# The end of the gated mixers: where the merged columns are transposed, and the output projection's first tiles

## The chip, the cores and the metric

The kernel runs on one core of a Trainium2 chip, in one launch. The core has TensorE (matmuls and transposes, PE in the profile), VectorE (DVE), ScalarE (ACT), GpSimd (POOL) and SyncE (SP), which here only issues DMAs. Each engine takes its instructions in the order in which they were written, and semaphores order them between engines. The metric is the device time of one execution in microseconds (us).

## The reference

Two residual networks follow each other on 256 tokens of 1,024 features in float32: first two layers with attention or retention between feed-forward blocks, then two layers of a gated mixer and an MLP. Cut to what the change touches, a layer of the second network is:

```
h = rmsnorm(x, g_mix[l])
dq, dk, dv, c_q, c_kv_kr, xq, gate_logits = split(h @ w_in[l])
y_diff = diff_attention(...) @ w_diff_o[l]
y_mla  = latent_attention(...) @ w_mla_o[l]
y_mem  = memory_cross_attention(...) @ w_cross_o[l]
gates = sigmoid(gate_logits + b_gate[l])
merged = gates[:, :, 0] * y_diff + gates[:, :, 1] * y_mla + gates[:, :, 2] * y_mem
x = x + merged @ w_out[l]
u = rmsnorm(x, g_mlp[l]) @ w_mlp1[l]
x = x + square(relu(u)) @ w_mlp2[l]
```

The change concerns `merged @ w_out[l]`, once in each of the two layers.

## The kernel before

**Tiles.** The 256 tokens stand in two halves of 128 rows. A weight matrix is streamed in tiles of 128 x 1,024 numbers. SyncE loads a tile into one of four buffers `w_raw`. ScalarE rounds it to `w_hi` (L1884), and VectorE or GpSimd makes `w_lo` = raw - hi (L2186 on VectorE, L2892 on GpSimd). There are four buffers of each, so a `w_hi` may be written when the tile four places back has been used. That pair of operations is the step `split`. While attention outputs are made and until the stage ends, every even tile's `w_lo` is GpSimd's.

**Blocks.** `block` computes 512 output columns (c is 0 or 1) for both halves, in PSUM banks. Each 128 x 128 piece costs three matmuls (L1605, L1606, L1607): input hi by weight hi, input hi by weight lo, input lo by weight hi. A tile holds two chunks of 128 input features, so it is 2 chunks x 2 halves x 3 = 12 matmuls of 512 columns. `w_mla_o` has 512 rows, so a block of it is two tiles; `w_out` has 1,024, so a block is four.

**Transposed inputs.** The left operand is kept transposed. A `turn` is four transposes on TensorE (L1694) of four chunks of one half, then `xt_hi` on ScalarE (L1914) and `xt_lo` on VectorE (L2214). A matmul waits for `xt_lo` of its chunk and half.

**Merging.** `merge` is called for the three branches in turn, n = 0, 1, 2; the last is `w_mla_o`. For each block and half VectorE multiplies the bank by the gate (L2850, or L2856 into a buffer `tmp`) and, for n = 1 and 2, adds it to `mx_merged` (L2861). The add for n = 2 completes `merged(half, c)`, of which there are four.

**The order.** One list of steps, the plan, is written by generators, and every engine's program goes through it in that order and picks what is its own. `tile` writes the matmuls of a tile, and `tile_used` behind it writes the `split` of the tile four places on. `second_part` is a hook: a pair of a tile count and a function. When the number of tiles reaches that count, `tile` writes the matmuls, then the tile's `split`, and then calls the function. Before, only `feed` uses it, which makes the normed and transposed input of a stage. `last_plain` is the output projection: a block for c = 0 and one for c = 1, and in the next stage the result is added to `x`. After `drive(projections(), ...)` the function `mix` writes the four turns of `mx_merged` and then the projection.

Of the kernel before, what the change touches and what calls it, by code (L numbers as in the profile page):

```python
# [16 lines left out]
P = 128  # L17
SEQ = 256
HALVES = SEQ // P
# [95 lines left out]
def column_blocks(n, start=0):  # L115
    return [(start + c, min(BLOCK, n - c)) for c in range(0, n, BLOCK)]
# [263 lines left out]
def drive(main, side=None, every=1, finish=True, steps=1):  # L380
    n = 0
    while True:
        try:
            next(main)
        except StopIteration as stop:
            result = stop.value
            break
        n += 1
        if side is not None and n % every == 0:
            for _ in range(steps):  # L390
                next(side, None)
    if side is not None and finish:
        for _ in side:
            pass
    return result


class Kernel:
# [869 lines left out]
    def mix(self, layer, _):  # L1268
        a, L, small = self.a, f"{layer}", self.small_of
# [39 lines left out]
        def projections():  # L1309
            part = lambda name, dst, after=(): self.project(self.xt, w_in, D, IN_SIZES[name], dst, IN_AT[name], after)  # L1310
            got["cq"] = yield from part("cq", low[:, :, 0:MLA_QL], self.tok_after[0])
            got["ckv"] = yield from part("ckv", low[:, :, CKV_AT:D], self.tok_after[0])
            got["q"] = yield from part("dq", q)
            for c0, m in column_blocks(D):
                got["k", c0] = yield from self.block(self.xt, w_in, D, IN_AT["dk"] + c0, m)
            got["v"] = yield from part("dv", v)
            yield from need("low_t", "ckt")
            got["mq"] = yield from self.project(low_t, a["w_mla_qb_2"][layer], MLA_QL, MLA_H * MLA_QK, mq)
            got["kv"] = yield from self.project(low_t, a["w_mla_kvb_2"][layer], MLA_KVL, MLA_H * PER_KV, kv, first=MLA_QL // P)
            got["low", "over"] = self.last_tile()  # L1320
            got["xq"] = yield from part("xq", xq, [got["low", "over"]])
            yield from need("qt")
            yield from gate(0)
            yield from need("kt")
            yield from gate(1)
            yield from need("cqt", "mkt")
            yield from gate(2)
            self.xt_after = [self.last_tile()]
            yield from merge(0, 0, diff_t, "w_diff_o_2", D, 0)
            yield from merge(1, 2, mc_t, "w_cross_o_2", CROSS_H * CROSS_D, 4)  # L1330
            yield from merge(2, 1, mc_t, "w_mla_o_2", MLA_H * MLA_V, 0)
# [7 lines left out]
            self.step("next_gain", gi + 2, [("gate_bias", layer, g, HALVES - 1, D - BLOCK)])  # L1339

        merged = self.put("mx_merged" + L, 24, [P, HALVES, D])

        def merge(n, g, xt, name, rows, first):
            while any((int(xt is mc_t), first + i) not in turned_out for i in range(rows // P)):
                yield IDLE
            for half in range(HALVES):
                self.step("sigmoid", layer, g, half, gates[g][:, half, :])
            for c, (c0, m) in enumerate(column_blocks(D)):
                b = yield from self.block(xt, a[name][layer], rows, c0, m, first)
                for half in range(HALVES):  # L1350
                    self.step("merge", layer, n, half, c, b, merged[:, half, c0:c0 + m], gates[g][:, half, c0:c0 + m], g)
# [164 lines left out]
        prepared = together(memory_keys(), diff_keys(), diff_queries(), latent(), latent_keys(), cross_queries(), diff_outputs())  # L1516
        side = self.in_step(prepared, outputs())
        drive(projections(), side, finish=False)
        merged_t = Transposed("merged" + L, *self.xt_parts)

        for c in range(2):
            for half in range(HALVES):
                self.turn(lambda h, s: merged[:, h, s * P:(s + 1) * P], merged_t, half, [(4 * c + j, 4 * c + j) for j in range(4)],
                          [("merged", layer, half, c)], self.xt_after)
        self.tok_after = [[("turned", self.uid)]] * HALVES
        drive(self.last_plain(merged_t, a["w_out_2"][layer], D))


# [1519 lines left out]
```

## Time and profile before

| | us |
|---|---|
| median of 3 runs | 2480.88 |
| lowest and highest | 2477.91 and 2481.13 |
| the profiled execution | 2485.56 |
| its span in the trace | 2484.2 |
| TensorE busy in it | 2396.5 |
| VectorE busy | 1521.6 |
| ScalarE busy | 1187.6 |
| GpSimd busy | 283.8 |

The trace is of the one profiled execution, and its span leaves out 1.4 us around it. Times in it count from the span's start. Matmuls are pipelined, so one is listed as longer than the distance to the next, and a wait is what is left between a modelled end and the next start. The granted clock is 1.00 where TensorE has its full 2.4 GHz and 0.50 at 1.2 GHz. A line such as "[0.99 <-DVE mx_merged L2861]" says that the engine stood idle for 0.99 us until VectorE's write of `mx_merged`. The code's end of mixer 0 lies at 1715 to 1740 us of the span and that of mixer 1 at 2257 to 2282 us.

### The profile page before, as it was taken

The page shows a single profiled execution, that of the slowest core. Times are in us where ns is not written, and L with a number is a line of the kernel's source. Part 1 is how long each engine was busy: PE and PEld are TensorE (multiplying, and loading weights), DVE is VectorE, ACT ScalarE, POOL GpSimd, SP SyncE. Part 2 cuts the span into 40 slices and gives each one's busy share as a digit, 9 for nine tenths or more (in the row PEclk, how much of TensorE's full clock was granted, in tenths as well). Part 3 has the DMA queues.
Part 4 walks back from the last instruction along what each step waited for, and adds up shares of the span by engine and source line. Part 5 has one row for each costly group of instructions (what it writes and reads, how often), then busy time and mean ns, then how long its engine had stood idle before and what let it go on. Part 6 is the DMA issues. An engine that isn't in the chain of part 4 may idle for free.

```text
span 2484.2 us, 34969 instructions
## 1 busy us (share of the span) xinstructions
PE 2396.5 (96%) x14214; PEld 2060.9 (83%) x14214; DVE 1521.6 (61%) x2325; ACT 1187.6 (48%) x1782; POOL 283.8 (11%) x247
## 2 busy tenths in 40 slices
PE   8998999889999999999999998999999998999999
PEld 8986787779979977777898786787998876887997
DVE  6555556776556657666655677655665686656654
ACT  4443454344444445444444455554554555554543
POOL 1100010000000000000000121333100122333000
PEclk9999999999999999999999999999999999999999
DMA  7754544446656555544566554445566553445564
GB/s 225 198 200 152 165 127 139 126 146 193 187 171 186 181 192 177 170 137 152 166 183 212 180 170 129 119 126 166 175 196 203 181 156 117 119 144 161 168 187 146
DMA packets 269424, 411.69 MB, mean 166 GB/s; under 512 B 13770, under 2 KB 141658, under 8 KB 269264
## 3 DMA queue, kind: packets, MB, share of 16 engines
q1 hardware_dynamic: 262400, 389.59, 51.5%
q0 software_dynamic: 6432, 19.28, 2.9%
q8 instruction: 112, 1.84, 0.3%
q10 hardware_dynamic: 432, 0.59, 0.1%
q14 instruction: 48, 0.39, 0.0%
HBM read 408.31 MB, written 1.10 MB: 165 GB/s over the span
## 4 chain that ended last, share of the span: by engine, by line
PE 76%; DVE 14%; ACT 6%; issue 2%; POOL 1%; DMA 0%; SPq 0%; ACTq 0%; DVEq 0%
PE banks L1605 14%; PE banks L1607 14%; PE banks L1606 13%; PE banks L1631 10%; PE banks L1640 9%; PE banks L1632 9%; DVE w_lo L2186 3%; ACT w_hi L1884 3%; PE banks L1754 1%; DVE probs L2373 1%; ACT probs L1992 1%; PE banks L1694 1%; PE banks L1707 1%; POOL stat L2873 1%; DVE mx_merged L2861 1%
## 5 line engine op out<-in xcount | busy, mean ns | idle before, releaser
L2186 DVE TENSOR_TENSOR w_lo<-w_raw,w_hi 128x1024 fp32r<-128x1024 f32 x688 | 837.7, 1224 | 706.2 <-ACT w_hi L1884 703.8
L1884 ACT ACTIVATE w_hi<-w_raw 128x1024 fp32r<-128x1024 f32 (+2 forms) x744 | 776.2, 1049 | 569.1 <-PE banks L1607 420.5
L1631 PE MATMUL banks<-xt_hi,w_hi 128*128 128x256 f32 x1920 | 477.9, 287 | 12.2 <-ACT xt_hi L1914 8.9
L1632 PE MATMUL banks<-xt_hi,w_lo 128*128 128x256 f32 x1920 | 475.4, 282 | 0.0
L1605 PE MATMUL banks<-w_hi,xt_hi 128*128 128x512 f32 (+2 forms) x1088 | 450.7, 414 | 12.1 <-DVE xt_lo L2214 4.4
L1607 PE MATMUL banks<-w_hi,xt_lo 128*128 128x512 f32 (+2 forms) x1088 | 430.2, 395 | 0.0
L1606 PE MATMUL banks<-w_lo,xt_hi 128*128 128x512 f32 (+2 forms) x1088 | 429.9, 395 | 0.0
L1631 PEld LDWEIGHTS banks<-xt_hi,w_hi 128*128 128x128 f32 x1920 | 364.2, 190 | 16.2 <-issue 12.6
L1632 PEld LDWEIGHTS banks<-xt_hi,w_lo 128*128 128x128 f32 x1920 | 367.3, 191 | 0.0
L1640 PE MATMUL banks<-xt_lo,w_hi 128*128 128x256 f32 x1920 | 270.3, 283 | 0.0
L1605 PEld LDWEIGHTS banks<-w_hi,xt_hi 128*128 128x128 f32 x1088 | 208.6, 192 | 60.2 <-issue 8.3
L1607 PEld LDWEIGHTS banks<-w_hi,xt_lo 128*128 128x128 f32 x1088 | 207.9, 191 | 47.9
L1640 PEld LDWEIGHTS banks<-xt_lo,w_hi 128*128 128x128 f32 x1920 | 247.5, 189 | 0.0
L1606 PEld LDWEIGHTS banks<-w_lo,xt_hi 128*128 128x128 f32 x1088 | 209.0, 192 | 44.1 <-issue 3.1
L2873 POOL TENSOR_TENSOR stat<-stat,minus_half 128x1 f32<-128x1 f32 (+2 forms) x60 | 53.4, 896 | 1055.2 <-DVE stat L2273 712.1
L2892 POOL TENSOR_TENSOR w_lo<-w_raw,w_hi 128x1024 fp32r<-128x1024 f32 x56 | 134.1, 2394 | 299.2 <-ACT w_hi L1884 299.2
L1605 PE MATMUL banks<-w_hi,ffn_ht_hi 128*128 128x512 f32 x352 | 140.7, 400 | 0.0
L1607 PE MATMUL banks<-w_hi,ffn_ht_lo 128*128 128x512 f32 x352 | 138.7, 394 | 0.0
L1606 PE MATMUL banks<-w_lo,ffn_ht_hi 128*128 128x512 f32 x352 | 138.1, 392 | 0.0
L1605 PE MATMUL banks<-w_hi,mlp_ht_hi 128*128 128x512 f32 x256 | 102.4, 400 | 0.0
L1607 PE MATMUL banks<-w_hi,mlp_ht_lo 128*128 128x512 f32 x256 | 100.8, 394 | 0.0
L1606 PE MATMUL banks<-w_lo,mlp_ht_hi 128*128 128x512 f32 x256 | 100.4, 392 | 0.0
(399 smaller groups left out, 2825.7 us busy)
## 6 DMA issues: line engine op xcount, KB each, us to landing
w_raw<-in_w_mlp SPq DMA_DIRECT2D x128, 512.0 KB, 3.7
w_raw<-in_w_in SPq DMA_DIRECT2D x104, 512.0 KB, 3.7
w_raw<-in_ffn_w_gate SPq DMA_DIRECT2D x88, 512.0 KB, 4.0
w_raw<-in_ffn_w_up SPq DMA_DIRECT2D x88, 512.0 KB, 4.1
w_raw<-in_ffn_w_down SPq DMA_DIRECT2D x88, 512.0 KB, 3.6
w_raw<-in_attn_w_in SPq DMA_DIRECT2D x72, 512.0 KB, 3.8
w_raw<-in_ret_w_in SPq DMA_DIRECT2D x64, 512.0 KB, 3.8
w_raw<-in_ret_w_out SPq DMA_DIRECT2D x16, 512.0 KB, 3.7
```

Source lines behind the costliest of these rows:

```text
L1605: pe.matmul(bank, xh, wh, start=(c == 0), stop=False)
L1606: pe.matmul(bank, xh, wl, start=False, stop=False)
L1607: mm = pe.matmul(bank, xl, wh, start=False, stop=(c == b.chunks - 1))
L1631: pe.matmul(out[f], hi[:, cols], xh, start=(c == 0), stop=False)
L1632: pe.matmul(out[f], lo[:, cols], xh, start=False, stop=False)
L1640: mm = pe.matmul(out[f], hi[:, cols], xl, start=False, stop=(c == DC - 1))
L1694: mm = pe.transpose(bank[:, j * P:(j + 1) * P], t.src(t.half, s), order)
L1707: mm = pe.transpose(bank[0:z.shape[-1], at:at + P], z, order)
L1884: act.activation(k.w_hi[i % SPLIT][:, 0:m], k.raw[i % RAW][:, 0:m], ACT.Copy).then_inc(*ev.mark(k.w_hi_made, ("w_hi", i)))
L2186: dve.tensor_tensor(lo, raw, hi.bitcast(F32), ALU.subtract).then_inc(*ev.mark(k.w_lo_made, ("w_lo", i)))
L2873: pool.tensor_tensor(out, mean, k.minus_half[:, 0:n], ALU.pow).then_inc(*ev.mark(k.pool_done, name))
L2892: pool.tensor_tensor(lo, raw, hi.bitcast(F32), ALU.subtract).then_inc(*ev.mark(k.w_lo_pool, ("w_lo", i)))
```

## The change

The four turns of `mx_merged` are the same instructions as before, in two pairs at other places. The pair for c = 0 is hooked to the first tile of the last merging block (n = 2, c = 1), so it stands between that block's two tiles. The pair for c = 1 is hooked to the second tile of the output projection. The object `merged_t` and the function that writes a pair move ahead of `merge`. `tok_after`, which says from when `tok` may be written again, is set with each pair, so the last one holds, as before.

```
--- before.py
+++ after.py
@@ -1339,6 +1339,13 @@
             self.step("next_gain", gi + 2, [("gate_bias", layer, g, HALVES - 1, D - BLOCK)])
 
         merged = self.put("mx_merged" + L, 24, [P, HALVES, D])
+        merged_t = Transposed("merged" + L, *self.xt_parts)
+
+        def merged_turned(c):
+            for half in range(HALVES):
+                self.turn(lambda h, s: merged[:, h, s * P:(s + 1) * P], merged_t, half, [(4 * c + j, 4 * c + j) for j in range(4)],
+                          [("merged", layer, half, c)], self.xt_after)
+            self.tok_after = [[("turned", self.uid)]] * HALVES
 
         def merge(n, g, xt, name, rows, first):
             while any((int(xt is mc_t), first + i) not in turned_out for i in range(rows // P)):
@@ -1346,6 +1353,8 @@
             for half in range(HALVES):
                 self.step("sigmoid", layer, g, half, gates[g][:, half, :])
             for c, (c0, m) in enumerate(column_blocks(D)):
+                if n == 2 and c == 1:
+                    self.second_part = len(self.tiles) + 1, lambda: merged_turned(0)
                 b = yield from self.block(xt, a[name][layer], rows, c0, m, first)
                 for half in range(HALVES):
                     self.step("merge", layer, n, half, c, b, merged[:, half, c0:c0 + m], gates[g][:, half, c0:c0 + m], g)
@@ -1516,13 +1525,7 @@
         prepared = together(memory_keys(), diff_keys(), diff_queries(), latent(), latent_keys(), cross_queries(), diff_outputs())
         side = self.in_step(prepared, outputs())
         drive(projections(), side, finish=False)
-        merged_t = Transposed("merged" + L, *self.xt_parts)
-
-        for c in range(2):
-            for half in range(HALVES):
-                self.turn(lambda h, s: merged[:, h, s * P:(s + 1) * P], merged_t, half, [(4 * c + j, 4 * c + j) for j in range(4)],
-                          [("merged", layer, half, c)], self.xt_after)
-        self.tok_after = [[("turned", self.uid)]] * HALVES
+        self.second_part = len(self.tiles) + 2, lambda: merged_turned(1)
         drive(self.last_plain(merged_t, a["w_out_2"][layer], D))
```

In the lists below, names end in the buffer's number: `w_hi_53` to `w_hi_56` with `w_lo_57` to `w_lo_60` are the four weight buffers, `mx_merged_228` is layer 0's merged tensor, `mx_mc_t` is the transposed input of the last merging blocks and `xt` the transposed `mx_merged`. The lines of the changed kernel are three higher, since its code is longer.

TensorE before, from the last matmuls of the merging block's last tile to the projection's first tile:

```order
L1605 MATMUL banks<-w_hi_56,mx_mc_t_hi 128x512
L1606 MATMUL banks<-w_lo_60,mx_mc_t_hi 128x512
L1607 MATMUL banks<-w_hi_56,mx_mc_t_lo 128x512
L1694 MATMUL banks<-ident,mx_merged_228 128x128 x16
L1605 MATMUL banks<-w_hi_53,xt_hi 128x512
L1606 MATMUL banks<-w_lo_57,xt_hi 128x512
L1607 MATMUL banks<-w_hi_53,xt_lo 128x512
```

TensorE now, at the first pair of turns, between the two tiles of the last merging block:

```order
L1608 MATMUL banks<-w_hi_55,mx_mc_t_hi 128x512
L1609 MATMUL banks<-w_lo_59,mx_mc_t_hi 128x512
L1610 MATMUL banks<-w_hi_55,mx_mc_t_lo 128x512
L1697 MATMUL banks<-ident,mx_merged_228 128x128 x8
L1608 MATMUL banks<-w_hi_56,mx_mc_t_hi 128x512
L1609 MATMUL banks<-w_lo_60,mx_mc_t_hi 128x512
L1610 MATMUL banks<-w_hi_56,mx_mc_t_lo 128x512
```

and at the second pair, between the second and the third tile of the projection:

```order
L1608 MATMUL banks<-w_hi_54,xt_hi 128x512
L1609 MATMUL banks<-w_lo_58,xt_hi 128x512
L1610 MATMUL banks<-w_hi_54,xt_lo 128x512
L1697 MATMUL banks<-ident,mx_merged_228 128x128 x8
L1608 MATMUL banks<-w_hi_55,xt_hi 128x512
L1609 MATMUL banks<-w_lo_59,xt_hi 128x512
L1610 MATMUL banks<-w_hi_55,xt_lo 128x512
```

Eight of the sixteen transposes have moved ahead of a tile of twelve matmuls, and the other eight behind two tiles of the projection.

VectorE before, from the last adds for c = 0 (the third row completes half 1) to the next layer of splits:

```order
L2861 TENSOR_TENSOR mx_merged_228<-mx_merged_228,tmp_72 128x512
L2856 TENSOR_TENSOR tmp_73<-banks,mx_gate_210 128x512
L2861 TENSOR_TENSOR mx_merged_228<-mx_merged_228,tmp_73 128x512
L2186 TENSOR_TENSOR w_lo_60<-w_raw_52,w_hi_56 128x1024
L2856 TENSOR_TENSOR tmp_70<-banks,mx_gate_210 128x512
L2861 TENSOR_TENSOR mx_merged_228<-mx_merged_228,tmp_70 128x512
L2856 TENSOR_TENSOR tmp_71<-banks,mx_gate_210 128x512
L2861 TENSOR_TENSOR mx_merged_228<-mx_merged_228,tmp_71 128x512
L2214 TENSOR_TENSOR xt_lo<-banks,xt_hi 128x4x128 x4
L2186 TENSOR_TENSOR w_lo_58<-w_raw_50,w_hi_54 128x1024
L2186 TENSOR_TENSOR w_lo_60<-w_raw_52,w_hi_56 128x1024
```

VectorE now, over the same work:

```order
L2864 TENSOR_TENSOR mx_merged_228<-mx_merged_228,tmp_72 128x512
L2859 TENSOR_TENSOR tmp_73<-banks,mx_gate_210 128x512
L2864 TENSOR_TENSOR mx_merged_228<-mx_merged_228,tmp_73 128x512
L2217 TENSOR_TENSOR xt_lo<-banks,xt_hi 128x4x128 x2
L2189 TENSOR_TENSOR w_lo_60<-w_raw_52,w_hi_56 128x1024
L2859 TENSOR_TENSOR tmp_70<-banks,mx_gate_210 128x512
L2864 TENSOR_TENSOR mx_merged_228<-mx_merged_228,tmp_70 128x512
L2859 TENSOR_TENSOR tmp_71<-banks,mx_gate_210 128x512
L2864 TENSOR_TENSOR mx_merged_228<-mx_merged_228,tmp_71 128x512
L2189 TENSOR_TENSOR w_lo_58<-w_raw_50,w_hi_54 128x1024
L2217 TENSOR_TENSOR xt_lo<-banks,xt_hi 128x4x128 x2
L2189 TENSOR_TENSOR w_lo_60<-w_raw_52,w_hi_56 128x1024
```

Two `xt_lo` now stand ahead of `w_lo_60` (the split of the projection's fourth tile), and the other two stand behind `w_lo_58`, a split that the second tile's use releases.

On ScalarE, in the same way, two `xt_hi` have moved ahead of the split `w_hi_56` (the projection's fourth tile), and the other two stand behind `w_hi_54` of the projection's sixth tile. GpSimd's and SyncE's lists are unchanged.

## Rows read from the trace of the kernel before

**Rows 1.** the page's part 1, TensorE's busy time, share of the span, count
```profile
PE 2396.5 (96%) x14214; PEld 2060.9 (83%) x14214; DVE 1521.6 (61%) x2325; ACT 1187.6 (48%) x1782; POOL 283.8 (11%) x247
```

**Rows 2.** TensorE's waits: us in total, times, longest
```profile
PE banks L1694 <- DVE mx_merged L2861: 6.5, 6, 1.8
```

**Rows 3.** timeline of TensorE, layer 0: start, us busy, what, [idle before]
```profile
1717.95 0.39 PE L1605 MATMUL banks<-w_hi,mx_mc_t_hi 128*128 128x512 f32 x1
...
1720.75 0.60 PE L1694 MATMUL banks<-ident,mx_merged 128*128 128x128 f32 x4
1722.34 0.66 PE L1694 MATMUL banks<-ident,mx_merged 128*128 128x128 f32 x4 [0.99 <-DVE mx_merged L2861]
...
1726.12 0.73 PE L1694 MATMUL banks<-ident,mx_merged 128*128 128x128 f32 x4 [0.67 <-DVE mx_merged L2861]
1726.82 0.77 PE L1605 MATMUL banks<-w_hi,xt_hi 128*128 128x512 f32 x1
```

**Rows 4.** timeline of VectorE, layer 0
```profile
1718.75 0.69 DVE L2861 TENSOR_TENSOR mx_merged<-mx_merged,tmp 128x512 f32<-128x512 f32 x1
...
1720.08 2.20 DVE L2861 TENSOR_TENSOR mx_merged<-mx_merged,tmp 128x512 f32<-128x512 f32 x1
1722.21 1.21 DVE L2186 TENSOR_TENSOR w_lo<-w_raw,w_hi 128x1024 fp32r<-128x1024 f32 x1
...
1725.38 0.69 DVE L2861 TENSOR_TENSOR mx_merged<-mx_merged,tmp 128x512 f32<-128x512 f32 x1
1725.99 2.48 DVE L2214 TENSOR_TENSOR xt_lo<-banks,xt_hi 128x512 fp32r<-128x512 f32 x4
1735.30 1.23 DVE L2186 TENSOR_TENSOR w_lo<-w_raw,w_hi 128x1024 fp32r<-128x1024 f32 x1 [6.84 <-ACT w_hi L1884]
```

**Rows 5.** timeline of GpSimd, layer 0
```profile
1719.36 2.38 POOL L2892 TENSOR_TENSOR w_lo<-w_raw,w_hi 128x1024 fp32r<-128x1024 f32 x1 [2.92 <-ACT w_hi L1884]
```

**Rows 6.** timeline of ScalarE, layer 0
```profile
1718.21 1.07 ACT L1884 ACTIVATE w_hi<-w_raw 128x1024 fp32r<-128x1024 f32 x1 [1.74 <-PE banks L1607]
1721.01 1.06 ACT L1884 ACTIVATE w_hi<-w_raw 128x1024 fp32r<-128x1024 f32 x1 [1.73 <-PE banks L1607]
...
1723.03 0.60 ACT L1914 ACTIVATE xt_hi<-banks 128x512 fp32r<-128x512 f32 x1 [0.48 <-PE banks L1694]
...
1734.21 1.06 ACT L1884 ACTIVATE w_hi<-w_raw 128x1024 fp32r<-128x1024 f32 x1 [1.75 <-PE banks L1607]
```

**Rows 7.** timeline of VectorE, layer 1
```profile
2261.43 2.42 DVE L2861 TENSOR_TENSOR mx_merged<-mx_merged,tmp 128x512 f32<-128x512 f32 x1
```

**Rows 8.** windows: length, busy PE PEld DVE ACT POOL, clock, DMA, GB/s
```profile
1720.75:1726.82 6.07, 2.60 (x18) 1.65 (x16) 6.00 (x8) 2.73 (x4) 0.98 (x1) 0.98 0.72 212
1726.82:1739.57 12.75, 12.75 (x49) 10.20 (x49) 2.87 (x4) 3.78 (x4) 3.81 (x2) 0.88 0.28 85
...
2262.31:2268.46 6.15, 3.14 (x18) 2.26 (x16) 6.08 (x8) 2.74 (x4) 0.99 (x1) 0.79 0.68 218
2268.46:2281.70 13.24, 13.24 (x50) 10.60 (x49) 2.89 (x4) 3.78 (x4) 3.82 (x2) 0.84 0.24 74
```

**Rows 9.** windows over seven hand-overs of stages and the matmuls behind
```profile
211.10:218.53 7.43, 4.71 (x16) 3.59 (x17) 6.64 (x12) 2.26 (x5) 0.21 (x1) 0.73 0.22 72
530.65:538.11 7.46, 4.71 (x36) 4.27 (x37) 6.62 (x11) 2.14 (x3) 0.74 (x2) 1.00 0.21 70
728.86:735.74 6.88, 4.71 (x36) 4.26 (x37) 6.08 (x10) 2.14 (x3) 0.14 (x1) 1.00 0.21 80
926.49:932.72 6.23, 4.71 (x23) 3.63 (x24) 5.43 (x9) 2.14 (x3) 1.74 (x4) 1.00 0.43 158
1196.78:1204.23 7.45, 4.68 (x25) 4.27 (x25) 6.62 (x11) 2.14 (x3) 0.70 (x2) 0.78 0.23 72
1750.98:1757.23 6.25, 4.49 (x24) 4.05 (x23) 5.40 (x8) 2.14 (x3) 0.81 (x1) 0.73 0.34 108
2293.11:2299.35 6.24, 4.49 (x27) 4.05 (x25) 5.39 (x8) 2.14 (x3) 0.80 (x1) 0.78 0.32 102
```

## The prediction

> **What bounds the kernel now.** I read the page first: TensorE is busy 96% of the span [rows 1], so time is won or lost where TensorE waits. The list of its waits puts 6.5 us, in six waits, on the adds that finish `mx_merged` [rows 2]. There are two mixers, so this is one place that occurs twice. I then read TensorE's timeline there, in layer 0 [rows 3]. The last tile of the last block starts at 1717.95 and the next thing TensorE can do stands at 1720.75, so one tile is 2.80 us. Then come four turns of four transposes, the first two at 1720.75 and 1722.34, the last at 1726.12, each but the first behind an add. The output projection begins at 1726.82, 6.07 us after the tile's end.
>
> VectorE says why [rows 4]. It is behind by more than a tile. The adds of the first column block, `merged(0,0)` and `merged(1,0)`, start at 1718.75 and 1720.08, although that block's matmuls ended a tile before 1717.95, at 1715.15. The second of them takes 2.20 us in place of 0.69. GpSimd's low part `w_lo` runs from 1719.36 to 1721.74 [rows 5], and the add ends 0.54 us behind it, at 1722.28. In layer 1 the same add starts at 2261.43 and takes 2.42 us [rows 7], so this repeats. Behind it in VectorE's queue stand a `w_lo`, the merges of the second column block (done at 1726.07) and the four `xt_lo`.
>
> The rest of the cost is TensorE's clock. The windows [rows 8] show the stretch between last tile and projection (6.07 and 6.15 us) and the projection's four tiles behind it, 12.75 us at a mean clock of 0.88 and 13.24 us at 0.84. Four tiles at full clock are 4 x 2.80 = 11.2 us, so the low level of 1.2 GHz cost 1.55 and 2.04 us. From the last tile's end to the end of the four tiles it takes 6.07 + 12.75 = 18.82 us in layer 0 and 6.15 + 13.24 = 19.39 us in layer 1, together 38.21 us. The change is weighed against this.
>
> **The first pair of turns, now ahead of the last tile.** TensorE takes work in program order, so the last tile waits for both turns, and the second turn for `merged(1,0)`. Up to here nothing is changed: GpSimd's `w_lo` depends on the `w_hi` that ScalarE starts at 1718.21, when the tile ahead is used [rows 6], which stays. So I take 1722.28 as it is. The second turn starts at 1722.34, as it does now [rows 3], its four transposes take about 0.5 us (0.60 to 0.73 busy, overlapped by what follows), and the last tile starts at 1722.8 in place of 1717.95: **+4.85 us**. Layer 1 shows the same add ending at 2263.85 and gives 4.83. Before, these 2.80 us of matmuls covered most of the late adds; the change takes that cover away.
>
> In exchange the projection starts right behind the last tile. Its first two tiles need only the first four chunks. `xt_hi` of half 1 takes 0.60 us from 1723.03 [rows 6] and `xt_lo` by another 0.7, near 1724.4, ahead of the last tile's end at 1725.6. So the 6.07 us vanish, and nothing is late there.
>
> **The second pair of turns, behind two tiles of the projection.** Call the last tile's new end 0. `w_lo` of the projection's fourth tile stands ahead of the second merges on VectorE and needs ScalarE's `w_hi`, which starts 0.26 after the tile (1721.01 less 1720.75, [rows 3, 6]) and lets VectorE start 1.09 later (1735.30 less 1734.21, [rows 4, 6]). The merges then take some 2.7 us and the last add would start at 4.4. GpSimd's next `w_lo` would start at 0.26 + 2.80 + 1.15 = 4.2 [rows 5, 6], so this add is held as now: it ends at 4.2 + 2.38 + 0.54 = 7.1. The turns can start at 5.6, when the two tiles end, and the second one at 7.2. That is not what ends last. The tile's own `w_hi` and `w_lo` were put ahead of `xt_hi` and `xt_lo` in both queues: `w_hi` starts 0.26 after the second tile and frees VectorE's `w_lo` at 1.35, which takes 1.21 [rows 4]; `xt_lo` takes 0.62 (2.48 for four, [rows 4]), and TensorE follows 0.06 later. That is 3.24 us, and up to 0.1 more since the held add ends just behind its `w_hi`: **3.3 us** (3.2 to 3.4) in which TensorE does eight transposes. The third tile's `w_hi` and `w_lo` are long made.
>
> From the old end of the last tile to the end of the four tiles it is now 4.85 + 11.2 + 3.3 = 19.35 us a layer at full clock, 38.7 us for both, **+0.5 us**. The two waits that replace the one are together about as long.
>
> **The clock.** What was one stretch of 6 us a layer with little but transposes is two, of 4.85 and 3.3 us. The nearest rows are seven places where a stage hands over to the next, with eight transposes and no other matmul of weights in them [rows 9]. Each row takes in 3.4 us of matmuls behind the hand-over, so the hand-overs are 2.8 to 4.1 us long. Behind four of them the clock falls (means of 0.73, 0.78, 0.73, 0.78), behind three, one of them 4.06 us long (7.46 less 3.40), it doesn't. 7.43 x 0.27, 7.45 x 0.22, 6.25 x 0.27 and 6.24 x 0.22 are 2.0, 1.6, 1.7 and 1.4 us; with the 1.55 and 2.04 above I take 1.65 us for each fall. Both 6 us stretches at this place have a fall in or behind them, so I give the new 4.85 us stretch 0.85 and the 3.3 us stretch 0.57 (4 of 7): 2 x 0.85 + 2 x 0.57 = 2.8 falls. With three it is 38.7 + 3 x 1.65 = 43.65 us against 38.21: **+5.4 us**.
>
> The Trainium skill has a rule that is harder on this change: TensorE: Matmul & The Clock Gate, Part 4: PE-mode transpose, says that transposes don't count as activity for the clock as matmuls do. By it every one of the four stretches is as good as idle and the clock would fall behind all: +7.1 us. The trace agrees only in part, since three of seven such stretches in rows 9 kept 1.00.
>
> **The rivals.**
> - All four stretches cost a fall: 38.7 + 6.6 - 38.21, +7.1 us. For it: rows 9 with 2.85 us already had one. Against it: three stretches without.
> - Only the first stretch of each layer does: 38.7 + 3.3 - 38.21, +3.8 us, within the bound below.
> - Not slower: the clock stays high at three or all of the four places. That is +0.5 to +2.1 us. It decides at how the transposes split the wait: by the times above the longest unbroken wait in any of them is 2.2 us, from the first turn's end near 1720.1 to 1722.34. The same page of the Trainium skill, Why this matters for your kernels, only warns of long unbroken idle gaps, and by it the clock would stay high here. Against it: the two waits of 1.80 us at most [rows 2] that ended in a fall in both layers.
> - The add is not held by GpSimd in its new surroundings. It would end at 1720.08 + 0.69 = 1720.77, and the last tile start 1.5 us earlier, 3.0 us for both: +2.4 us. Everything ahead of the add is unchanged, so I hardly believe it.
> - The change does what its form suggests: the merged columns are ready within the last block. All waits and falls would go, 38.21 less 2 x (11.2 + 2.0 for sixteen transposes) or 12 us at most. For that `merged(1,0)` would have to end by 1717.95, and it ends 4.3 us later.
>
> **How the numbers follow.** The profiled execution is 2485.56 us with a span of 2484.2; its ends are untouched, so differences carry over to the median of 2480.88 us, 4.7 lower. Three falls (forecast): 0.32, 2486.3 us, and its own range is 2484.5 to 2488. All four: 0.25, 2488.0. Two: 0.25, 2484.7. None or one: 0.07, 2481.4 to 2483.0. Add not held: 0.04, 2483.3. Ready in time: 0.07, down to 2469. The measurement tells about 0.2%, 5.0 us, from no change. Slower by more: three quarters of 0.32 (5.4 is just over the bound), nearly all of 0.25 and a sixth of the next, 0.51. Faster by more: 0.07. The rest, 0.42, is within. The range 2481.6 to 2489.3 leaves out the last case and the tails.
>
> **What would show it.** TensorE should show a wait of some 1.4 us and then one of some 2.2 us, both on an add of `mx_merged`, ahead of the last tile of the block; no wait at the projection's first tile; and at its third tile a wait on `xt_lo` of some 1.3 us behind the last turn. VectorE should show `w_lo` ahead of that `xt_lo`. The add of 2.20 us should still be long and end 0.5 us behind GpSimd. The count of stretches at half clock between the last block and the projection's end should be three of four. I am wrong if the adds come earlier than they do now, if the first wait is shorter than 4 us in all, or if the number of falls is another.

## The result and the profile after

| | median us | lowest to highest | executions |
|---|---|---|---|
| before | 2480.51 | 2476.8 to 2485.7 | 6 |
| the change | 2489.72 | 2488.7 to 2490.46 | 6 |

The ratio is 1.0037 with an interval of 1.0024 to 1.0050: the change is slower, by about 9 us. A repeated comparison, with 11 executions of the change against 29 of before (x9 below), gave 1.0019 (1.0011 to 1.0028), 4.7 us. The sign holds in both; the size lies between 3 and 12 us, and both intervals contain 1.0024 to 1.0028, some 6 to 7 us. The prediction said 2486.3 us, within 2481.6 to 2489.3, so the first median is 0.4 us above its range.

The profiled execution of the change took 2490.44 us with a span of 2489.1, 4.9 above the span of before. Its busy times, for [rows 1]:

```profile
PE 2397.9 (96%) x14214; PEld 2062.4 (83%) x14214; DVE 1526.3 (61%) x2325; ACT 1188.4 (48%) x1782; POOL 284.1 (11%) x247
```

The work is the same in number. The waits of TensorE on the adds of `mx_merged`, for [rows 2], have grown from 6.5 to 9.1 us (total, times, longest):

```profile
PE banks L1697 <- DVE mx_merged L2864: 9.1, 6, 2.3
```

TensorE's timeline at the end of mixer 0, for [rows 3] (start, us busy, what, [idle before]):

```profile
1719.17 0.40 PE L1610 MATMUL banks<-w_hi,mx_mc_t_lo 128*128 128x512 f32 x1
1721.06 0.63 PE L1697 MATMUL banks<-ident,mx_merged 128*128 128x128 f32 x4 [1.49 <-DVE mx_merged L2864]
...
1723.75 0.66 PE L1697 MATMUL banks<-ident,mx_merged 128*128 128x128 f32 x4 [2.07 <-DVE mx_merged L2864]
1724.17 0.48 PE L1608 MATMUL banks<-w_hi,mx_mc_t_hi 128*128 128x512 f32 x1
...
1727.05 0.40 PE L1608 MATMUL banks<-w_hi,xt_hi 128*128 128x512 f32 x1
...
1734.26 0.66 PE L1697 MATMUL banks<-ident,mx_merged 128*128 128x128 f32 x4 [1.00 <-DVE mx_merged L2864]
...
1736.09 0.47 PE L1608 MATMUL banks<-w_hi,xt_hi 128*128 128x512 f32 x1 [1.17 <-DVE xt_lo L2217]
```

Two waits, 1.49 and 2.07, stand ahead of the last tile of the block (1724.17). The projection starts at 1727.05 without a wait. Its third tile waits 1.17 for `xt_lo`, behind a turn that has itself waited 1.00. That is the shape that the prediction drew. VectorE shows the reason of each, for [rows 4]:

```profile
1721.55 2.15 DVE L2864 TENSOR_TENSOR mx_merged<-mx_merged,tmp 128x512 f32<-128x512 f32 x1
...
1731.59 2.62 DVE L2864 TENSOR_TENSOR mx_merged<-mx_merged,tmp 128x512 f32<-128x512 f32 x1
1734.13 1.21 DVE L2189 TENSOR_TENSOR w_lo<-w_raw,w_hi 128x1024 fp32r<-128x1024 f32 x1
1735.27 1.27 DVE L2217 TENSOR_TENSOR xt_lo<-banks,xt_hi 128x512 fp32r<-128x512 f32 x2
```

and GpSimd, for [rows 5]:

```profile
1720.80 2.35 POOL L2895 TENSOR_TENSOR w_lo<-w_raw,w_hi 128x1024 fp32r<-128x1024 f32 x1 [2.90 <-ACT w_hi L1887]
...
1731.26 2.39 POOL L2895 TENSOR_TENSOR w_lo<-w_raw,w_hi 128x1024 fp32r<-128x1024 f32 x1 [8.11 <-ACT w_hi L1887]
```

Both long adds end behind GpSimd: at 1723.70, 0.55 after 1723.15, and at 1734.21, 0.56 after 1733.65. `w_lo` at 1734.13 stands ahead of `xt_lo` at 1735.27.

ScalarE's `w_hi` mark the tiles' ends (0.26 us before them, as in [rows 6]):

```profile
1719.67 1.06 ACT L1887 ACTIVATE w_hi<-w_raw 128x1024 fp32r<-128x1024 f32 x1 [1.74 <-PE banks L1610]
1727.31 1.06 ACT L1887 ACTIVATE w_hi<-w_raw 128x1024 fp32r<-128x1024 f32 x1 [2.26 <-PE banks L1610]
1732.93 1.06 ACT L1887 ACTIVATE w_hi<-w_raw 128x1024 fp32r<-128x1024 f32 x1 [1.74 <-PE banks L1610]
```

The first two are 7.64 apart, of which a tile is 2.80, so the first wait costs 4.84. The second tile of the projection ends at 1732.93 - 0.26 = 1732.67 and the third starts at 1736.09: 3.42 us.

The windows that answer to [rows 8] run from the last tile's old end, 2.80 behind the first `w_hi` less 0.26, to the end of the projection's four tiles, in layer 0 and in layer 1 (length, busy PE PEld DVE ACT POOL, clock, DMA share, GB/s):

```profile
1722.21:1741.79 19.58, 15.87 (x73) 12.65 (x74) 10.86 (x11) 6.04 (x8) 4.75 (x3) 1.00 0.40 126
2264.57:2288.09 23.52, 19.83 (x72) 15.70 (x73) 10.84 (x11) 5.92 (x7) 4.74 (x3) 0.78 0.34 104
```

Layer 0 never left the full clock and took 19.58 us, against 18.82 before with its fall in it. Layer 1 took 23.52 against 19.39. The waits there are alike (1.25, 2.30, 0.98 and 1.17), so nearly all of the 3.94 us between the layers is the low level of the clock. It stood there in two stretches, the first and the third of these rows:

```profile
2264.20:2271.80 7.60, 5.69 (x16) 4.67 (x17) 3.15 (x3) 0.84 (x2) 1.31 (x1) 0.55 0.40 126
2271.80:2281.80 10.00, 7.85 (x37) 6.09 (x36) 8.06 (x8) 4.26 (x5) 2.39 (x1) 0.99 0.36 108
2281.80:2285.00 3.20, 3.20 (x8) 2.44 (x8) 0.00 (x0) 0.00 (x0) 0.00 (x0) 0.50 0.50 158
```

**One measure for all kernels.** For the experiments I take the whole place, in each layer: from the first matmul on `mx_mc_t`, where the second of the three branches begins to be merged, to the first matmul of the next stage. Before, the change, and each of them a second time (x10, x9); the rows stand in the order before, x10, change, x9, two layers each:

```profile
1698.35:1753.83 55.48, 50.26 (x218) 39.62 (x216) 34.19 (x36) 24.27 (x27) 20.18 (x9) 0.97 0.52 160
2239.92:2295.95 56.03, 51.28 (x217) 40.63 (x216) 34.27 (x36) 24.16 (x27) 20.19 (x9) 0.94 0.52 159
```

```profile
1698.83:1754.41 55.58, 50.31 (x217) 39.66 (x216) 34.20 (x36) 24.27 (x27) 20.19 (x9) 0.97 0.51 160
2240.57:2296.71 56.14, 51.36 (x218) 40.66 (x216) 34.30 (x36) 24.16 (x27) 20.19 (x9) 0.94 0.52 158
```

```profile
1699.81:1756.04 56.23, 48.75 (x217) 38.45 (x216) 36.17 (x36) 24.27 (x27) 20.12 (x9) 1.00 0.51 158
2242.17:2302.35 60.18, 52.72 (x218) 41.50 (x216) 36.16 (x36) 24.15 (x27) 20.15 (x9) 0.91 0.48 148
```

```profile
1697.96:1757.07 59.11, 51.65 (x217) 40.72 (x216) 36.16 (x36) 24.26 (x27) 20.13 (x9) 0.94 0.49 151
2241.70:2302.00 60.30, 52.86 (x217) 41.60 (x216) 36.15 (x36) 24.15 (x27) 20.14 (x9) 0.92 0.50 147
```

Both layers together are 111.5 and 111.7 us before, 116.4 and 119.4 with the change. The first difference, 4.9, is also the difference of the two spans, so the rest of the program took the same time in sum; not in each part, since the stretch ahead of the place is 1.46 us longer with the change (1699.81 against 1698.35) and the one behind it 1.50 shorter (186.75 against 188.25). The spans of the second pair differ by 5.3 (2490.3 and 2485.0), so there the rest took 2.4 us less. The second difference, 7.7, has the same waits (1.48, 2.08, 0.98, 1.17 in layer 0) and differs from the first by what the clock did in layer 0, 1.00 there and 0.94 here. x9 has four low stretches, behind or in each pair's wait in both layers, where the first trace has two, both in layer 1:

```profile
1721.90:1725.40 3.50, 3.50 (x11) 2.97 (x12) 1.24 (x2) 0.60 (x1) 0.00 (x0) 0.53 0.51 150
1734.90:1738.90 4.00, 3.18 (x8) 2.54 (x9) 1.27 (x3) 0.28 (x1) 0.00 (x0) 0.57 0.75 243
2264.00:2271.60 7.60, 5.96 (x17) 4.85 (x18) 2.88 (x3) 0.60 (x1) 1.03 (x1) 0.55 0.36 116
2281.40:2284.80 3.40, 3.40 (x10) 2.71 (x9) 0.00 (x0) 0.00 (x0) 0.00 (x0) 0.52 0.54 153
```

### The profile page after: what moved, and what is told of

The parts are those of the page before. It is cut to its first block, busy times and chain, and to the rows that moved or that the text cites. A ratio compares the mean times of both kernels' runs of the same rounds, so it can differ in the third digit from the quotient of the medians.

```text
span 2489.1 us, 34969 instructions
## 1 busy us (share of the span) xinstructions
PE 2397.9 (96%) x14214; PEld 2062.4 (83%) x14214; DVE 1526.3 (61%) x2325; ACT 1188.4 (48%) x1782; POOL 284.1 (11%) x247
## 4 chain that ended last, share of the span: by engine, by line
PE 76%; DVE 14%; ACT 6%; issue 2%; POOL 1%; DMA 0%; SPq 0%; ACTq 0%; DVEq 0%
PE banks L1608 14%; PE banks L1610 13%; PE banks L1609 13%; PE banks L1635 9%; PE banks L1634 9%; PE banks L1643 9%; DVE w_lo L2189 3%; ACT w_hi L1887 3%; PE banks L1757 1%; DVE probs L2376 1%; ACT probs L1995 1%; PE banks L1697 1%; PE banks L1710 1%; DVE mx_merged L2864 1%; POOL stat L2876 1%
```

## The experiments

The medians are compared with executions of the kernel before on the same chip in the same session: 25 in the first (median 2487.46), 35 in the second (2484.71), 29 in the third (2483.56). x1 to x4 are of the first, x5 to x8 of the second, x9 to x12 of the third, and the three sessions ran on three chips. A difference in us is the ratio less one, times 2483. "Place" is the sum of the measure above over both layers, against 111.5 to 111.7 before.

**x1, only the first pair moved.** The second pair stands ahead of the whole projection:

```
-        self.second_part = len(self.tiles) + 2, lambda: merged_turned(1)
+        merged_turned(1)
         drive(self.last_plain(merged_t, a["w_out_2"][layer], D))
```

> The first pair of turns stands in the last merging block, as in the change; the second pair stays ahead of the whole projection, as before. Theory of the queues: the last tile starts 4.85 us later, as in the change, and the projection's first tile then waits for the last add (0.26 + 1.09 for w_hi, then w_lo and the four merging operations, 5.1 us) and its turn, 5.65 us. From the old end of the last tile to the end of four tiles that is 4.85 + 5.65 + 11.2 = 21.7 us a layer at full clock against 17.3 before, +8.9 us for both layers, and with two falls of the clock more than before +12 us; in any case slower than the change by 4 to 5 us. Rival, that the clock's falls are the whole loss and each pair brings its own: half of the change's loss, +4.6 us.

2500.87 us, ratio 1.0054 (1.0037 to 1.0070), +13.4; place 125.2, at clocks 0.92 and 0.89. The first wait of the change is there, and so is the old one, now of 3.79 us and at the low level of the clock (four transposes took 1.11 us in place of 0.66):

```profile
1734.70 1.11 PE L1697 MATMUL banks<-ident,mx_merged 128*128 128x128 f32 x4 [3.79 <-DVE mx_merged L2864]
```

As expected. The first pair pays for itself only if the projection can then start at once.

**x2, only the second pair moved.**

```
-                if n == 2 and c == 1:
-                    self.second_part = len(self.tiles) + 1, lambda: merged_turned(0)
...
+        merged_turned(0)
         self.second_part = len(self.tiles) + 2, lambda: merged_turned(1)
```

> The first pair stays behind the last merging block and its merges, as before; the second pair stands behind two tiles of the projection, as in the change. Theory of the queues: the first tile of the projection still waits 6.0 us, since its xt_lo stands behind all merges on VectorE, and the third tile waits 3.3 to 3.4 us, since w_hi and w_lo of a later tile stand ahead of xt_hi and xt_lo. That is 6.0 + 11.2 + 3.3 = 20.5 us a layer against 17.3, +6.4 us, and with one more fall of the clock +8 us (6 to 10). TensorE's wait ahead of the third tile should be on xt_lo and 1.1 to 1.3 us long. Rival, that the second pair is free and the first pair is all of the loss: no slower than before, -1 to +1 us.

2493.83 us, 1.0033 (1.0021 to 1.0044), +8.2; place 121.6, clocks 0.94 and 0.92.

```profile
1729.49 0.55 PE L1607 MATMUL banks<-w_hi,xt_hi 128*128 128x512 f32 x1 [3.83 <-DVE xt_lo L2216]
...
1736.72 1.03 PE L1696 MATMUL banks<-ident,mx_merged 128*128 128x128 f32 x8
...
1740.05 0.77 PE L1607 MATMUL banks<-w_hi,xt_hi 128*128 128x512 f32 x1 [2.29 <-DVE xt_lo L2216]
```

The wait of 2.29 is longer than the 1.1 to 1.3 expected because the turns no longer wait; the third tile comes 3.33 us behind the second (1740.05 - 1736.72), as the theory of the queues has it. The two halves cost 13.4 and 8.2, the whole 4.7 to 9.2: they don't add, since each half alone keeps a wait that the other removes.

**x3, the change with the second pair's turns written ahead of that tile's split.**

```
         if self.second_part and len(self.tiles) == self.second_part[0]:
-            self.tile_used(used)
+            ahead = len(self.second_part) == 3
+            if not ahead:
+                self.tile_used(used)
             self.second_part[1]()
+            if ahead:
+                self.tile_used(used)
...
+        self.second_part = len(self.tiles) + 2, lambda: merged_turned(1), True
```

> The change with one thing altered: the second pair of turns is written ahead of the second tile's split, so that xt_hi and xt_lo stand ahead of that split's w_hi and w_lo. Theory of the queues: the third tile starts 2.3 us behind the second tile's end (the held add at 7.1 is then what ends last) in place of 3.4, 1.1 us less a layer and 2.2 us for both, and a shorter stretch makes a fall of the clock rarer, another 0 to 2 us: the change less 2 to 4 us, +5 to +7 us against before. Rival, that the held add and not the split is what the third tile waits for: as the change, +9 us.

2485.73 us, 0.9997 (0.9986 to 1.0008), -0.7, no difference from before where +5 to +7 was expected; place 114.4. The wait on `xt_lo` at the third tile is gone, and only the one on the add (0.99) is left: the tile starts 2.28 us behind the second one's end (1738.33 - 1736.05) in place of 3.42. So the 3.3 us were set by `w_hi` and `w_lo` of the tile's own split standing ahead, as the prediction said, and their order is worth 1.1 us a layer at full clock. The place is still 2.9 us longer than that of before; that the medians don't show it goes with the executions of before in the first session, which had more of the low clock than any other set (28.9 us in the table below).

**x4 and x5, no low parts on GpSimd from the second branch on**, in the change and in before; VectorE makes those eight `w_lo` a layer too.

```
             yield from merge(0, 0, diff_t, "w_diff_o_2", D, 0)
+            self.share = 0
```

> The change, but from the second and third merged branch on VectorE makes every w_lo and GpSimd none. Theory: GpSimd's w_lo holds one add of VectorE in each pair of tiles for 1.5 to 2 us and so puts it behind. Without it merged(1,0) ends 5.2 us after the block's matmuls in place of 7.1, the last tile starts 2.9 us late in place of 4.85, 3.9 us less for both layers, 5 to 6 with rarer falls: +3 to +5 us against before in place of +9. No add of mx_merged is longer than 0.75 us. Rival, that VectorE is behind by its own work and one w_lo more only adds to it: as the change or 1 to 2 us slower, +9 to +11 us.

> The kernel before, with every w_lo from the second merged branch on made by VectorE. Theory: merged(1,0) is ready before the last tile ends, but the first tile still waits for w_lo, four merging operations and xt_lo behind that tile, 5.9 us in place of 6.07. So -0.3 us for both layers at full clock, and within 2 us of the kernel before. Rival, that the held adds set the time before too: 1.5 us less a layer, -3 us.

x4: 2489.24 us, 1.0010 (1.0000 to 1.0020), +2.5; place 110.3, clocks 0.99. x5: 2487.58 us, 1.0014 (1.0003 to 1.0024), +3.5; place 112.8. In x4 all sixteen adds are short (min/median/max ns), and the waits of the first pair fall from 1.49 and 2.07 to 1.09 and 0.61:

```profile
L2865 DVE TENSOR_TENSOR mx_merged<-mx_merged,tmp x16: 691/692/694, 1706.9 to 2270.7; 128x512 f32<-128x512 f32 x16
```

```profile
1718.90 0.63 PE L1698 MATMUL banks<-ident,mx_merged 128*128 128x128 f32 x4 [1.09 <-DVE mx_merged L2865]
...
1720.14 0.66 PE L1698 MATMUL banks<-ident,mx_merged 128*128 128x128 f32 x4 [0.61 <-DVE mx_merged L2865]
```

That GpSimd's operation holds the add is shown. But the kernel isn't faster for it than before, and x5, where I expected a difference within 2 us of none, is slower. A part of what VectorE pays for the eight `w_lo` stands at the end of the place: in x4, x5, x8 and x12 TensorE waits twice a layer for VectorE's `tok`, the next stage's input; in before, the change, x3 and x11 it waits there once, 0.97 or 0.98 us. In layer 0 of x12:

```profile
1749.91 0.66 PE L1702 MATMUL banks<-ident,tok 128*128 128x128 f32 x4 [0.99 <-DVE tok L2202]
1751.24 0.66 PE L1702 MATMUL banks<-ident,tok 128*128 128x128 f32 x4 [0.67 <-DVE tok L2202]
```

That is 0.7 us a layer, 1.4 of the 3.5 us of x5. The rest is not assigned.

**x6 and x7, matmuls without use in the waits**, in the change and in before. They are listed as `banks<-causal,ident`; the numbers are how many stand ahead of each of the pair's two turns and behind them.

```
+FILLS = ((3, 5, 0), (0, 2, 3))
...
             for half in range(HALVES):
+                if FILLS[c][half]:
+                    self.step("fill", f"m{layer}{c}{half}", FILLS[c][half])
```

(x7: `((0, 2, 0), (5, 1, 0))`.)

> The change with matmuls of ident by causal (384 columns, thrown away) where TensorE waits: three and five ahead of the two turns of the first pair, two ahead of the second turn of the second pair and three behind it, 0.34 us each and so inside the waits of 1.4, 2.1, 1.0 and 1.2 us. Theory: the waits are set by other engines and stay, so at full clock the kernel still needs 19.5 us a layer against 17.3 before, but the clock falls behind none of the four stretches. It costs +4.5 us against a before without falls; against the measured before, which has about one or two falls there, +1.5 to +3 us, 5 to 7 us faster than the change. Rival, that falls are not what makes the change 9 us slower: as the change, +9 us, or slower by the fillers.

> The kernel before with the same kind of fillers in its waits: two ahead of the second turn, five ahead of the third, one ahead of the fourth. Theory: the falls of the clock go, and with them 1.65 us each. If the kernel before has a fall in each layer in most executions, -3.3 us; if its profiled execution, 5 us above its median, was one with more falls than usual, -1 to -2 us. The difference between the filled change and this one is that of the waits alone, 4.5 us.

x6: 2489.24 us, 1.0019 (1.0008 to 1.0030), +4.7; place 116.2. x7: 2481.46 us, 0.9990 (0.9979 to 1.0002), -2.5, which can't be told from none; place 109.6. They lie 7.2 us apart where 4.5 was expected. The low clock is gone from the place in both, in both layers (layer 0 of each):

```profile
1693.43:1751.53 58.10, 56.26 (x244) 43.33 (x242) 36.16 (x36) 24.28 (x27) 20.14 (x9) 1.00 0.51 154
```

```profile
1699.47:1754.27 54.80, 53.05 (x233) 41.46 (x232) 34.38 (x36) 24.27 (x27) 20.21 (x9) 1.00 0.52 161
```

But they are too many. In x6 the place is 1.87 us a layer longer than the undisturbed layer of the change (58.10 against 56.23), so what the clock gave back went into the fillers. In x7 this can be read from TensorE: from the first turn to the projection it is 1728.70 - 1721.87 = 6.83 us in place of 6.07, 0.76 more.

```profile
1721.87 0.60 PE L1701 MATMUL banks<-ident,mx_merged 128*128 128x128 f32 x4
...
1728.70 0.48 PE L1612 MATMUL banks<-w_hi,xt_hi 128*128 128x512 f32 x1
```

This gives a clean size. A layer of before without any fall is 54.80 - 0.76 = 54.04 us, a layer of the change without any is 56.23. (The layers of before less the 1.55 and 2.04 us that the prediction took for their falls give 53.93 and 53.99.) **The change costs 2.19 us a layer, 4.4 in all, at the same clock.** Of the 7.2 us between x6 and x7 the fillers are 2 x (1.87 - 0.76) = 2.2. The place of before is 111.5, so its falls cost 111.5 - 108.1 = 3.4 us; those of the change cost 116.4 - 112.5 = 3.9 and, in x9, 6.9.

**x8 and x12 (the same kernel), the cover kept.** The first pair one tile later, behind the last tile; both pairs ahead of their split; no low parts on GpSimd:

```
                 if n == 2 and c == 1:
-                    self.second_part = len(self.tiles) + 1, lambda: merged_turned(0)
+                    self.second_part = len(self.tiles) + 2, lambda: merged_turned(0), True
...
-        self.second_part = len(self.tiles) + 2, lambda: merged_turned(1)
+        self.second_part = len(self.tiles) + 2, lambda: merged_turned(1), True
```

> A version drawn from the theory: no pair stands ahead of a tile that could run. The first pair stands behind the last merging block's last tile but ahead of its merges, the second behind two tiles of the projection, both ahead of the split of the tile before them, and VectorE makes every w_lo from the second merged branch on. Theory: the first tile starts 2.1 us behind the last (now 6.07) and the third 2.1 us behind the second, 2.1 + 11.2 + 2.1 = 15.4 us a layer against 17.3, -3.8 us, and stretches of 2.1 us that are half transposes bring no fall of the clock, another -2 to -3.5 us: -5 to -7 us against before. Rival, that VectorE without GpSimd falls behind: the first tile waits for late adds and it is no faster than before.

> The version with kept cover and without GpSimd again, on the same chip as the change and the version with GpSimd. Theory: -4 to -6 us against before, 10 to 14 us faster than the change, no fall of the clock at the end of either mixer and waits of 1.07 us ahead of the projection's first and third tile.

x8: 2480.25 us, 0.9984 (0.9975 to 0.9994), -4.0, where -5 to -7 was expected. x12: 2480.21 us, 0.9985 (0.9976 to 0.9993), -3.7, where -4 to -6 was. Place 106.3 in both. What is left is a wait of 1.07 us on `xt_lo` behind each pair, and the clock stays at 1.00 or 0.99:

```profile
1721.82 0.47 PE L1613 MATMUL banks<-w_hi,xt_hi 128*128 128x512 f32 x1 [1.07 <-DVE xt_lo L2222]
```

**x11, the same with GpSimd's low parts kept.**

> The version with kept cover (first pair behind the last merging block's last tile and ahead of its merges, second pair behind two tiles of the projection, both ahead of the split), but GpSimd keeps its w_lo. Theory: the late add ends 1.6 us behind the last tile as before, so the second turn starts there and the projection's first tile 2.3 us behind the last tile, 0.2 us later than without GpSimd; the rest is the same: -3.5 to -6 us against before, and the same as the version without GpSimd within 1 us. Rival, that the gain came from taking GpSimd away: -1 us or less.

**2476.94 us, 0.9968 (0.9956 to 0.9980), -7.9 us: it beats both kernels.** Expected was the time of x12 within 1 us; the median, of five executions only, is 3.3 us below that of x12. The intervals of the two overlap (0.9956 to 0.9980 and 0.9976 to 0.9993), so the size of this difference is uncertain. Layer 0 of x11, then of x12:

```profile
1698.01:1750.59 52.58, 48.80 (x217) 38.37 (x216) 36.23 (x36) 24.17 (x27) 20.18 (x9) 1.00 0.55 170
```

```profile
1699.53:1752.68 53.15, 48.57 (x218) 38.49 (x216) 36.76 (x44) 23.94 (x27) 1.00 (x1) 1.00 0.57 173
```

The place is 105.2 against 106.3, which explains 1.1 of the 3.3 and nearly all of the 1.2 us between the two profiled spans (2477.4 and 2478.6). Against before the place is 6.3 us shorter: 2.9 at full clock (52.58 and 52.60 against 54.04) and the 3.4 of the falls, which are gone. The held adds are still there, and in layer 0 each pair waits 0.99 and 0.97 for one, but they now lie behind the tile instead of ahead of it:

```profile
1721.99 0.66 PE L1701 MATMUL banks<-ident,mx_merged 128*128 128x128 f32 x4 [0.99 <-DVE mx_merged L2868]
...
1729.95 0.66 PE L1701 MATMUL banks<-ident,mx_merged 128*128 128x128 f32 x4 [0.97 <-DVE mx_merged L2868]
```

**x9 and x10, the change and before, unaltered.**

> The change itself once more, for a second trace and more executions. Theory: the waits repeat to 0.1 us in both layers (two ahead of the last tile, 4.85 us in all, 3.4 us ahead of the third tile), since they don't hang on the clock; the falls of the clock don't repeat: zero and one long one in the first trace, two to four here, each 1.7 us. From the first matmul of the last merging blocks to the next stage's first matmul 56.2 us a layer without falls and 58 to 60 with. Against before +5 to +9 us. Rival, that the first comparison was drawn high by the small number of executions of before: +3 us or less.

> The kernel before against itself: what a difference of nothing looks like here, and a second trace. Theory: its times spread over 12 us (2477 to 2489) because the number of falls of the clock differs from execution to execution, so the ratio is 1.000 within 0.0012. In the end of each mixer the same three waits on adds, and one or two falls.

x9: 2488.55 us (2484.72 to 2491.62), 1.0019 (1.0011 to 1.0028). The waits repeat as expected, and there are four low stretches; the first trace has two, not the one long one that is said above. x10: 2482.95 us (2476.82 to 2488.74), 1.0000 (0.9989 to 1.0011). Before against itself shows no difference, as it should, but its own executions lie 12 us apart.

**Where the spread comes from.** Of most executions the span and its mean granted clock are recorded. Span times clock is what would be left at full clock if the whole span shrank with the clock; the rest is at most what the low level cost (less where TensorE only waited). Means, each good to about 1 us:

| kernel, session | executions | span | span x clock | rest |
|---|---|---|---|---|
| before, first | 25 | 2484.3 | 2455.4 | 28.9 |
| before, second | 35 | 2482.8 | 2455.5 | 27.2 |
| before, third | 29 | 2482.3 | 2455.6 | 26.7 |
| the change, first result | 6 | 2488.4 | 2461.0 | 27.4 |
| x9, the change | 11 | 2487.4 | 2461.2 | 26.2 |
| x10, before | 12 | 2482.3 | 2455.4 | 26.9 |
| x3 | 11 | 2483.6 | 2458.5 | 25.1 |
| x4 | 12 | 2487.2 | 2459.7 | 27.6 |
| x5 | 12 | 2486.1 | 2459.5 | 26.5 |
| x6 | 12 | 2487.3 | 2465.5 | 21.8 |
| x7 | 12 | 2479.8 | 2460.0 | 19.8 |
| x8 | 12 | 2478.6 | 2455.8 | 22.7 |
| x12 | 11 | 2479.2 | 2454.6 | 24.6 |
| x11 | 5 | 2474.9 | 2455.1 | 19.8 |

The full-clock part of before is the same to 0.3 us in four sets, on three chips. Its executions differ by what the clock does: in the third set the quickest two have 0.992, the slowest two 0.988 and 0.987. The full-clock part of the change is 5.5 and 5.6 above before. The measure is good for sets of one kernel and rough between kernels: a wait at the low level doesn't get shorter at full clock, but half of it is booked to the rest. The stretch of 6.15 us at 0.79 in layer 1 of before books 1.3 us to the rest, and is only 0.08 longer than that of layer 0, 6.07 at 0.98. So the full-clock part of x7 is 4.5 above before, though its fillers add only 1.5, and that of x11 only 0.5 below, though its place is 2.9 shorter without falls. For the six executions of before beside the first result the clocks aren't recorded. If they had the same 2455.5, their mean span of 2479.1 leaves 23.6 us of low clock, 3 to 5 less than in the other sets of before.

## Why the prediction was right in sign and short in size

**The first wait, +4.85 a layer: right.** Measured 4.84 in layer 0, and in layer 1, where four of the transposes ran at the low clock, 5.11. The add ended 0.55 us behind GpSimd (0.54 was taken), and x4 shows by its absence that it is GpSimd's operation which holds it. The rival in which the add is no longer held, and the one in which the columns are ready in time, fell with it.

**The third tile 3.3 us behind the second: right, 0.1 us short.** Measured 3.42 and, in layer 1, 3.41. The held add was forecast to end 7.1 us behind the last tile and ended 7.2 (1734.21 - 1727.05). x3 shows that the split ahead of the turns was the last link.

**No wait at the projection's start: right**, 1727.05 has none.

**The sum, 19.35 a layer at full clock: 19.58** in the layer that kept it.

**"The two waits that replace the one are together about as long": wrong as a reading, though not in its number.** The 19.35 us at full clock were set against 18.82 and 19.39 that had a fall in them. At the same clock the terms are 4.85 + 3.3 against 6.07, 2.1 us a layer more (2.0 against the 6.15 of layer 1), 4.1 in all; x7 and the change's layer 0 measured 4.4. The prediction's total has it, but books it to the clock: of its +5.4 us only 1.4 belong there, the change from falls of 1.55 + 2.04 to three of 1.65, and 4.1 to the waits. Where the clock falls as often after as before, the change still costs 4.4 us; the rival with one fall a layer has nearly this number (+3.8), but none of them named the waits as its cause.

**Three falls of 1.65 us: wrong in both traces, and right only as their mean, which is luck.** The prediction named another number of falls as a sign of being wrong. The first trace has two, both in layer 1, and x9 has four. They cost 3.9 us in one and 6.9 in the other, 2.4 and 4.2 times 1.65. Falls differ in length too (7.6 us at 0.55 behind the first pair of layer 1, 3.2 at 0.50 behind the second), so one price for each was too simple. Against the 3.4 and 3.6 of before in the paired traces the clock's share at this place is +0.5 or +3.3, where +1.4 was forecast; over all executions it can't be told from none (26.2 and 27.4 against 26.7 to 28.9). The rival "all four" is what x9 shows in number; "only the first of each layer" is seen in no trace of the change, but in both layers of x3, which has a shorter second stretch (clocks 0.97 and 0.94).

**"Differences carry over to the median of 2480.88 us, 4.7 lower": the step that failed.** A median of three executions was taken for the kernel's time, and the 4.7 us by which it lies below the profiled execution were taken off the forecast. The runs show no such gap: the change's profiled execution took 2490.44 us, within 0.5 of 2485.56 + 5.4 = 2491.0, and its six executions have a median only 0.7 below that. The medians of before in the three later sessions are 2487.46, 2484.71 and 2483.56, and one kernel's executions spread over 12 us; with these bases +5.4 gives 2489.0 to 2492.9. The size of the change was forecast as +5.4 and measured as +4.9 and +7.7 at the place, +4.7 by the larger comparison and +9.2 by the smaller. That the first comparison is 4 us above the larger one, and the median thus above the range, would follow if its six executions of before were a favourable draw of the clock (23.6 us of it by the estimate under the table); since their clocks aren't recorded, this last step is inferred and not shown. Nor is it known on which chip they ran, and a difference between chips or sessions is not ruled out: the later sets of before ran on three. The range had room for four unknown falls at one place, but none for the clock in the rest of the program.

**The clock rules.** Layers with the same waits (at most 2.08 in x9's layer 0 and in the change's) once fell and once did not, so neither one wait nor the transposes decide alone. By the Trainium skill (TensorE: Matmul & The Clock Gate, Part 4: PE-mode transpose) transposes don't count as activity in the way that matmuls do, and the prediction read it so that the clock falls behind every such stretch. The traces agree only in part: x9 has a fall at all four, but the change's layer 0 kept 1.00 behind stretches of 4.84 and 3.42 us with eight transposes each. In x8 and x12 each pair is 2.1 us of eight transposes and a wait of 1.07, and the place kept 0.99 or 1.00 in both layers of both traces. The same page of the Trainium skill (TensorE: Matmul & The Clock Gate, Why this matters for your kernels) warns only of long unbroken idle gaps, by which the prediction had the clock stay high. The measurement decides against that: in layer 1 of the change the clock fell 0.8 us into the second wait (2263.81 to 2266.11; the window 2264.50:2265.00 has a mean of 0.62), with a wait of 1.25 and four transposes ahead of it.

## What to carry to other kernels

Put a step that waits for a late result behind the work that covers the lateness, not ahead of it, and write it ahead of the refills of that work in every queue it goes through; x11 did both with the same idea as the change and gained 7.9 us where the change lost 5 to 9. Compare before and after at the same clock first, and price the clock apart from that. Where the clock's falls vary between executions, a median of three is no base to within 4 us: take many, and the clock of each with its time.

## What the hardware showed that I had not expected

- The same program spread over 12 us in 2480 (0.5%) while its full-clock part stayed within 0.3 us on average over four sets. In the profiled executions too: the change's layer 0 at 1.00 once and 0.94 once, with waits equal to 0.01 us.
- With short matmuls in the waits the clock stayed high: in the traces of x6 and x7 it was 1.00 throughout the place in both layers, and over the whole span the rest in the table fell by some 7 us for x7 although only 5 us of it (111.5 at 0.97 and 0.94) had been in the place. Why it fell elsewhere is open.
- Freeing VectorE's adds from GpSimd made neither kernel faster than before (x4 +2.5, x5 +3.5), though the place of x4 is 2.2 us shorter than the change's at full clock (110.3 against 112.5). Giving the work back to GpSimd gained 3.3 us by the medians (x11 against x12), only 1.1 of it seen in the place. The other 2.2 are within what the clock does between sets (24.6 and 19.8 us of rest), and I can't assign them.
